# A hybrid four-layer kernel: the rotary halves of queries and keys by DMA instead of by a permutation product

## The chip, the cores and the metric

The kernel runs on one core of a Trainium2 chip. The metric is the device time of one execution in microseconds, over repeated runs. The engines that matter are TensorE (PE, with its weight loads PEld), VectorE (DVE), ScalarE (ACT), GpSimd (POOL) and SyncE (SP), which issues the weight stream. ACT can issue DMAs too, from its own queue.

## The reference, cut to what matters

Two blocks of two layers each, on 256 tokens of width 1024, in float32. The change touches the two layers of the first block, in the attention branch:

```python
def partial_rope(t, cos, sin):
    half = ROT_DIM // 2                    # ROT_DIM = 16, so 8
    t1, t2, rest = tf[..., :half], tf[..., half:ROT_DIM], tf[..., ROT_DIM:]
    out = jnp.concatenate([t1 * c - t2 * s, t2 * c + t1 * s, rest], axis=-1)

for i in range(DEPTH):                     # DEPTH = 2
    h = rmsnorm(x, norm_mix[i])
    proj = h @ w_in[i]
    q, k, v, cb, cc, cx, u, g = jnp.split(proj, IN_SPLITS, axis=-1)
    q = partial_rope(q.reshape(b, l, N_Q_HEADS, HEAD_DIM), cos, sin)   # 8 heads of 64
    k = partial_rope(k.reshape(b, l, N_KV_HEADS, HEAD_DIM), cos, sin)  # 2 heads of 64
    y_attn = sliding_window_attention(q, k, v, attn_sinks[i]) @ w_attn_o[i]
    ...                                    # a convolution branch, a state-space branch, gates, FFN
```

Of the 64 dimensions of each head the first 16 are rotated: the first eight are mixed with the second eight.

## The kernel before, in words

**The weight stream.** All weights pass through as "slabs" of 128 partitions by 1024 columns (512 KB), in the order of use. SP loads a slab into one of four slots of `w_raw`. ACT copies it to `w_hi` (L1310, float32r), DVE computes the rest `w_lo = w_raw - w_hi` (L1811), and PE multiplies with both: 24 products of 128x128 by 128x256 a slab (L777 to L779: high times high, high times low, low times high). ACT and DVE make slab i+3 while they are at position i of their own list, and PE waits for `w_lo` of a slab before its first product. SP reloads a slot when `w_lo` of its slab is made.

**The order of the work.** Each of the first two layers has a table `ORDER1[n]`: after slab i come the tasks listed under i. PE, ACT and DVE each walk the same list in order and do their own share of each task, so the place of a task in the table decides what stands in front of and behind it on every engine. Nothing is reordered at run time.

**The attention part.** Slabs 0 to 4 give four tiles of queries (two heads each) and one of keys; ACT evacuates each into `qk[:, b, :]`, heads along the partitions, tokens along the columns. PE then multiplies each of the five tiles with the matrix `rope_r` (L997, task `("rope", b)`), which puts the turned halves (with their sign) on the first 16 partitions of each head and zeros elsewhere, in a PSUM bank. DVE (task `("rope_mul", b)`, L2146 to L2153) multiplies that with the sine table into `prob[:, b, :]`, the tile itself with the cosine table, and adds the two. `scaled_tables` (L2139) makes both tables, multiplied by the root of the norm, in `prob[:, 5]` and `prob[:, 6]`. Much later PE takes `qk` for the scores.

**Around it on DVE.** In the first layer: `root_of` (L1824 to L1828), the scaled activations (`work`, L1842), their low parts `h_lo` (L1848) and the `w_lo` of coming slabs. The first use of `h_lo` is slab 9 in the first layer and slab 5 in the second (`slab_normed`, L790 to L794: all high parts of x first, then the eight low ones). In the second layer the tasks `("power", p)` (L2115 to L2119) and the convolution (L2280 to L2291) share the same stretch. There is a loop between the engines: at each third slab of the convolution DVE makes `cy` (L2291), ACT makes `cv_hi` of it (L1525), and only then the next `w_hi`, for which DVE waits.

Of the kernel before, what the change touches and what calls it, by code (L numbers as in the profile page):

```python
# [44 lines left out]
SCORE_BANKS = 0, 1, 2  # L45
ROPE_BANKS = 2, 3, 0

# [48 lines left out]
for _name, _n in (("ones_d", P), ("ones_i", P), ("ident", P), ("g_mid", KD), ("g_final", KD),  # L96
                  ("rope_c", T), ("rope_s", T), ("rope_r", P), ("mask", TRI)):
    C1[_name] = (_at, _at + _n)
    _at += _n
# [21 lines left out]
def raw_end(n):  # L121
# [6 lines left out]
        3: (("mean",), ("roots",), ("h", 0), ("h", 1), ("h", 2), ("h", 3), ("lows",)),  # L128
        5: (("rope", 0),),
        6: (("rope", 1),),  # L130
        7: (("prep_d",), ("rope", 2)),
        9: (("scaled",),),
        10: (("rope_mul", 0),),
        12: (("out_table",),),
        14: (("power", 0),),
        15: (("rope", 3), ("rope_mul", 1)),
        17: (("rope", 4),),
        18: (("double", 0), ("double", 1)),
# [31 lines left out]
    },  # L170
    {
        1: (("mean",), ("roots",)),
        3: (("scaled",), ("h", 0), ("h", 1), ("h", 2), ("h", 3), ("lows",)),
        4: (("rope", 0), ("rope_mul", 0), ("rope", 1)),
        5: (("power", 0), ("rope_mul", 1)),
        7: (("rope", 2), ("rope", 3)),
        8: (("rope_mul", 2), ("power", 1)),
        9: (("rope_mul", 3), ("spread", 0), ("rope", 4)),
        10: (("rope_mul", 4), ("vt",), ("vt_copy",)),
        11: (("spread", 1), ("power", 2)),  # L180
# [142 lines left out]
def hybrid_kernel(nc, weights, x_t, p_d, c1_d, c2_d, decay_d, out_t):  # L323
    with ExitStack() as ctx:
# [211 lines left out]
        v_prep = sem("v_prep")  # L536
        pe_rope = sem("pe_rope")
        v_rope = sem("v_rope")
# [193 lines left out]
        def _(pe):  # L732
# [187 lines left out]
            def s5_turned(at, g):  # L920

                part, first = g // 4, 4 * (g % 4)
                if g == 0:
                    pe.wait_ge(v_power, at.n * 3 + 3)
                    pe.wait_ge(a_power, at.n * 2 + 2)
                if g < 4:
                    if g == 1:
                        pe.wait_ge(a_v, at.n + 1)
                    else:
                        pe.wait_ge(v_rope, at.n * 5 + (3, 0, 4, 5)[g])  # L930
                else:
                    pe.wait_ge(a_bt, at.n * 8 + (g - 3))
                for k in range(4):
                    last = nc.tensor.transpose(mid[g % 4][:, k * P:(k + 1) * P],
                                               bs[part][:, first + k, :, :].rearrange("p i c -> p (i c)"), con1("ident"))
                last.then_inc(pe_tr, 1)
# [50 lines left out]

            def rope(at, b):

                wait_out(pe, at, Q0 + b)  # L990
                if b == 0:
                    pe.wait_ge(tables_in, 16)
                if b == 2:
                    pe.wait_ge(v_norm, at.norm * 3 + 1)
                if b >= 3:
                    pe.wait_ge(v_rope, at.n * 5 + (b - 2))
                mm(mid[ROPE_BANKS[b % 3]][:, 0:T], con1("rope_r"), qk[:, b, :],  # L997
                   start=True, stop=True).then_inc(pe_rope, 1)

            def value_rows(at):  # L1000
# [6 lines left out]
            def scores(at, h):  # L1007

                a, g = h // 2, h % 2
                if h == 0:  # L1010
                    pe.wait_ge(v_rot, at.n * 4 + 4)
                elif h >= 3:
                    pe.wait_ge(v_mask, at.n * 8 + (h - 2))
                rows = slice(HD * g, HD * g + HD)
                dst = mid[SCORE_BANKS[h % 3]]
                mm(dst[:, 0:P], qk[rows, a, 0:P], qk[rows, 4, 0:P], start=True, stop=True)
                mm(dst[:, P:TRI], qk[rows, a, P:T], qk[rows, 4, :], start=True, stop=True).then_inc(pe_s, 1)
# [66 lines left out]
            for n in range(DEPTH):  # L1084
                at = Layer(False, n)
                for task in tasks1(n):
                    if task[0] == "slab":
                        first_slab(at, task[1])
                    elif task[0] == "mean":
                        mean(at, 0)  # L1090
                    elif task[0] == "rope":
                        rope(at, task[1])
                    elif task[0] == "tr":
# [210 lines left out]
        def _(act):  # L1304
# [194 lines left out]
            def mixed_high(at, n):  # L1499

                act.wait_ge(v_mg, at.n * 4 + (n + 1))
                nc.scalar.copy(h_hi[:, 2 * n:2 * n + 2, :], work[:, 2 * n:2 * n + 2, :]).then_inc(a_mhi, 1)

            def first_slab(at, i):
                if at.n or i + AHEAD > start_slabs:
# [70 lines left out]
            for n in range(DEPTH):  # L1576
                at = Layer(False, n)
                for task in tasks1(n):
# [12 lines left out]
                    elif task[0] == "lag_copy":  # L1591
                        lag_copy(at, task[1])
                    elif task[0] == "vt_copy":
                        act.wait_ge(pe_v, n + 1)
# [195 lines left out]
        def _(dve):  # L1790
# [355 lines left out]
            def rope(at, own, b):  # L2146

                dve.wait_ge(pe_rope, at.n * 5 + (b + 1))
                cos, sin = prob[:, 5, 0:T], prob[:, 6, 0:T]
                tt(prob[:, b, 0:T], mid[ROPE_BANKS[b % 3]][:, 0:T], sin, MUL)  # L2150
                tt(qk[:, b, :], qk[:, b, :], cos, MUL).then_inc(dve_step, 1)
# [210 lines left out]
            for n in range(DEPTH):  # L2362
                at = Layer(False, n)
                for task in tasks1(n):
# [28 lines left out]
                    elif task[0] == "out_power":  # L2393
                        out_power(at, own, task[1])
                    elif task[0] == "rope_mul":
                        rope(at, own, task[1])
# [508 lines left out]
```

## Time and profile before

| | |
|---|---|
| runs | 2137.98, 2138.44, 2140.2 us; median 2138.44 |
| the profiled execution | 2139.59 us, of which span 2137.80 us (1.79 us around it) |
| PE busy | 2113.5 us, 99% of the span |
| DVE busy | 1640.1 us, 77% |
| ACT busy | 1195.2 us, 56% |
| share of the chain that ended last | PE 89%, DVE 6%, ACT 2%, issue 2% |
| mean granted clock of PE | 0.997 |
| DMA | 385 MB, 180 GB/s over the span |

The busy share of PE is nearly full, since matmuls are pipelined and each is counted from its start to its modelled end. The chain that ended last tells more: it is followed back from the last instruction, at each step to what released it, and so shows in which stretches another engine than PE sets the time.

### The profile page before, as it was taken

Reading aid. Unit: us, or ns where it says so; the run is one execution under the profiler, and the core shown is the slowest. Engines: PE = TensorE matmul, PEld = TensorE weight load, DVE = VectorE, ACT = ScalarE, POOL = GpSimd, SP = SyncE. Lnnn points to the kernel's source line nnn. Section 1 sums busy time; section 2 is a strip of 40 time slices with the busy share of each in tenths; the row PEclk is TensorE's granted clock in tenths of the full one; section 3 lists DMA queues with packets and bytes.
Section 4 is the critical chain, followed back from the end, with each engine's and each line's share of the span. In section 5 each row is a group of like instructions: output and inputs, shape, how many; then the busy total and the mean of one; then the engine's idle time right before and its main releaser. Section 6 shows DMA issues by size and latency. Waiting matters only on the chain.

```text
span 2137.8 us, 47790 instructions
## 1 busy us (share of the span) xinstructions
PE 2113.5 (99%) x18652; PEld 2055.5 (96%) x18652; DVE 1640.1 (77%) x2620; ACT 1195.2 (56%) x1803; POOL 58.5 (3%) x54
## 2 busy tenths in 40 slices
PE   9999999999999999999999999999999999999998
PEld 8999999999999999899999999999899999999998
DVE  8987877987877776778957877776678947877764
ACT  6646644565555445546648745445446658845443
POOL 0000000000000000000002200000000002200000
PEclk9999999999999999999999999999999999999999
DMA  7434655654446556554455566556554556565553
GB/s 251 159 128 141 204 190 186 195 171 142 151 157 215 190 189 206 187 168 158 161 190 191 167 203 208 186 187 213 185 169 148 169 183 193 174 201 186 187 189 127
DMA packets 109984, 385.00 MB, mean 180 GB/s; under 512 B 12480, under 2 KB 16768, under 8 KB 109312
## 3 DMA queue, kind: packets, MB, share of 16 engines
q1 hardware_dynamic: 101664, 368.66, 52.2%
q10 hardware_dynamic: 8160, 14.04, 2.1%
q8 instruction: 121, 1.98, 0.4%
q14 instruction: 39, 0.32, 0.0%
HBM read 381.53 MB, written 1.11 MB: 179 GB/s over the span
## 4 chain that ended last, share of the span: by engine, by line
PE 89%; DVE 6%; ACT 2%; issue 2%; DMA 0%; DVEq 0%; ACTq 0%
PE acc L777 25%; PE acc L779 24%; PE acc L778 24%; DVE w_lo L1811 2%; PE acc L896 1%; PE acc L897 1%; PE acc L898 1%; PE acc L841 1%; PE acc L843 1%; PE acc L842 1%; ACT w_hi L1310 1%; PE mid L1133 1%; PE mid L1214 1%; DVE pr L2564 0%; PE mid L964 0%
## 5 line engine op out<-in xcount | busy, mean ns | idle before, releaser
L1811 DVE TENSOR_TENSOR w_lo<-w_raw,w_hi 128x1024 fp32r<-128x1024 f32 x694 | 848.5, 1227 | 306.8 <-ACT w_hi L1310 297.9
L1310 ACT CAST w_hi<-w_raw 128x1024 fp32r<-128x1024 f32 x694 | 724.7, 1047 | 541.3 <-PE acc L779 473.5
L777 PE MATMUL acc<-h_hi,w_hi 128*128 128x256 f32 x2096 | 599.4, 286 | 0.3 <-DVE w_lo L1811 0.3
L779 PE MATMUL acc<-h_hi,w_lo 128*128 128x256 f32 x2096 | 587.5, 280 | 0.0
L778 PE MATMUL acc<-h_lo,w_hi 128*128 128x256 f32 x2096 | 586.3, 280 | 0.0
L777 PE MATMUL acc<-g_hi,w_hi 128*128 128x256 f32 x1456 | 410.0, 282 | 0.8 <-DVE w_lo L1811 0.7
L779 PE MATMUL acc<-g_hi,w_lo 128*128 128x256 f32 x1456 | 407.2, 280 | 0.0
L778 PE MATMUL acc<-g_lo,w_hi 128*128 128x256 f32 x1456 | 406.8, 279 | 0.0
L777 PEld LDWEIGHTS acc<-h_hi,w_hi 128*128 128x128 f32 x2096 | 395.7, 189 | 7.7 <-issue 5.7
L779 PEld LDWEIGHTS acc<-h_hi,w_lo 128*128 128x128 f32 x2096 | 396.1, 189 | 0.0
L778 PEld LDWEIGHTS acc<-h_lo,w_hi 128*128 128x128 f32 x2096 | 395.1, 188 | 0.5
L777 PEld LDWEIGHTS acc<-g_hi,w_hi 128*128 128x128 f32 x1456 | 274.0, 188 | 2.0 <-DVE w_lo L1811 1.8
L779 PEld LDWEIGHTS acc<-g_hi,w_lo 128*128 128x128 f32 x1456 | 274.4, 188 | 0.0
L778 PEld LDWEIGHTS acc<-g_lo,w_hi 128*128 128x128 f32 x1456 | 273.4, 188 | 0.2
L777 PE MATMUL acc<-f_hi,w_hi 128*128 128x256 f32 x704 | 197.7, 281 | 0.2 <-DVE w_lo L1811 0.2
L779 PE MATMUL acc<-f_hi,w_lo 128*128 128x256 f32 x704 | 196.9, 280 | 0.0
L778 PE MATMUL acc<-f_lo,w_hi 128*128 128x256 f32 x704 | 196.7, 279 | 0.0
L777 PEld LDWEIGHTS acc<-f_hi,w_hi 128*128 128x128 f32 x704 | 132.5, 188 | 0.4 <-issue 0.4
L779 PEld LDWEIGHTS acc<-f_hi,w_lo 128*128 128x128 f32 x704 | 132.7, 188 | 0.0
L778 PEld LDWEIGHTS acc<-f_lo,w_hi 128*128 128x128 f32 x704 | 132.2, 188 | 0.0
L708 POOL TENSOR_TENSOR sqz<-xs 128x256 f32<-128x256 f32 x32 | 36.0, 1134 | 1800.6 <-DVE xs L2557 1800.4
L777 PE MATMUL acc<-r_hi,w_hi 128*128 128x256 f32 x256 | 73.4, 287 | 0.5 <-issue 0.5
(434 smaller groups left out, 3394.3 us busy)
## 6 DMA issues: line engine op xcount, KB each, us to landing
w_raw<-weights_d SPq DMA_DIRECT2D x695, 512.0 KB, 3.9
even<-rows_d ACTq DMA_DIRECT2D x16, 256.0 KB, 4.3
odd<-rows_d ACTq DMA_DIRECT2D x32, 128.0 KB, 3.4
p<-p_d ACTq DMA_DIRECT2D x3, 1080.0 KB, 8.5
rdec<-decay_d ACTq DMA_DIRECT2D x2, 768.0 KB, 5.3
p<-p_d SPq DMA_DIRECT2D x1, 1024.0 KB, 10.7
out_d<-work SPq DMA_DIRECT2D x4, 256.0 KB, 2.3
x_all<-x_d SPq DMA_DIRECT2D x1, 516.0 KB, 4.3
```

Of the source, the lines that this page charges most:

```text
L708: nc.gpsimd.tensor_tensor(sqz[:, b % 4, :], xs[:, b, :], xs[:, b, :], ALU.mult).then_inc(p_zsq, 1)
L777: mm(dst, wh, hi[:, k, :], start=first and j == 0, stop=False)
L778: mm(dst, wh, lo[:, k, :], start=False, stop=False)
L779: done = mm(dst, wl, hi[:, k, :], start=False, stop=last and j == len(ks) - 1)
L841: mm(dst, wh, hi[:, k, :], start=k == 0 and b == 0, stop=False, skip_group_check=True)
L842: mm(dst, wh, lo[:, k, :], start=False, stop=False, skip_group_check=True)
L843: done = mm(dst, wl, hi[:, k, :], start=False, stop=k == 3, skip_group_check=True)
L896: mm(dst, hh, wh, start=k == 0, stop=False)
L897: mm(dst, hh, wl, start=False, stop=False)
L898: done = mm(dst, hl, wh, start=False, stop=k == KD - 1)
L1310: nc.scalar.copy(w_hi[:, slot, :], w_raw[:, slot, :]).then_inc(hi_done, 1)
L1811: tt(w_lo[:, slot, :], w_raw[:, slot, :], w_hi[:, slot, :].bitcast(F32), SUB).then_inc(lo_v, 1)
```

## The change

The five products with `rope_r` of each layer go, and the matrix with them. In their place DVE clears `prob[:, 0:5, 0:256]` (one memset, task `("rope_zero",)`), ACT issues four DMAs (task `("rope_in",)`), each of which copies eight partitions of all five tiles of `qk` to `prob`, eight partitions further down or up. DVE reads the turned half from `prob` in SBUF and no longer from PSUM. The sign goes into the sine table. All five `rope_mul` tasks wait for all four DMAs. In the second layer the `rope_mul` tasks stand later: under slabs 8, 9, 10, 10 and 12, and no longer 4, 5, 8, 9 and 10. In the first layer they stay where they were. Four waits of PE on `v_rope` in `s5_turned` go, and PE's first score waits for it instead.

```diff
@@ ORDER1, first layer
         3: (("mean",), ("roots",), ("h", 0), ("h", 1), ("h", 2), ("h", 3), ("lows",)),
-        5: (("rope", 0),),
-        6: (("rope", 1),),
-        7: (("prep_d",), ("rope", 2)),
+        1: (("rope_zero",),),
+        6: (("rope_in",),),
+        7: (("prep_d",),),
         9: (("scaled",),),
         10: (("rope_mul", 0),),
         12: (("out_table",),),
         14: (("power", 0),),
-        15: (("rope", 3), ("rope_mul", 1)),
-        17: (("rope", 4),),
+        15: (("rope_mul", 1),),
@@ ORDER1, second layer
+        0: (("rope_zero",),),
         1: (("mean",), ("roots",)),
         3: (("scaled",), ("h", 0), ("h", 1), ("h", 2), ("h", 3), ("lows",)),
-        4: (("rope", 0), ("rope_mul", 0), ("rope", 1)),
-        5: (("power", 0), ("rope_mul", 1)),
-        7: (("rope", 2), ("rope", 3)),
-        8: (("rope_mul", 2), ("power", 1)),
-        9: (("rope_mul", 3), ("spread", 0), ("rope", 4)),
-        10: (("rope_mul", 4), ("vt",), ("vt_copy",)),
+        5: (("power", 0), ("rope_in",)),
+        8: (("rope_mul", 0), ("power", 1)),
+        9: (("rope_mul", 1), ("spread", 0)),
+        10: (("rope_mul", 2), ("rope_mul", 3), ("vt",), ("vt_copy",)),
+        12: (("rope_mul", 4),),
@@ PE, s5_turned
-                if g < 4:
-                    if g == 1:
-                        pe.wait_ge(a_v, at.n + 1)
-                    else:
-                        pe.wait_ge(v_rope, at.n * 5 + (3, 0, 4, 5)[g])
-                else:
+                    pe.wait_ge(v_norm, at.norm * 3 + 1)
+                elif g == 1:
+                    pe.wait_ge(a_v, at.n + 1)
+                if g >= 4:
                     pe.wait_ge(a_bt, at.n * 8 + (g - 3))
@@ PE
-            def rope(at, b):
-                ...
-                mm(mid[ROPE_BANKS[b % 3]][:, 0:T], con1("rope_r"), qk[:, b, :],
-                   start=True, stop=True).then_inc(pe_rope, 1)
@@ PE, scores
                 if h == 0:
+                    pe.wait_ge(v_rope, at.n * 5 + 5)
                     pe.wait_ge(v_rot, at.n * 4 + 4)
@@ ACT
+            def rope_rows(at):
+
+                for t in range(U0):
+                    wait_out(act, at, t)
+                act.wait_ge(v_rope_zero, at.n + 1)
+                for base in range(0, P, HD):
+                    for to, off in ((base, ROT // 2), (base + ROT // 2, -(ROT // 2))):
+                        act.dma_start(prob[to:to + ROT // 2, 0:U0, 0:T],
+                                      qk[to + off:to + off + ROT // 2, :, :]).then_inc(rope_in, 16)
@@ DVE, rope
-                dve.wait_ge(pe_rope, at.n * 5 + (b + 1))
+                dve.wait_ge(rope_in, (at.n + 1) * 4 * 16)
                 cos, sin = prob[:, 5, 0:T], prob[:, 6, 0:T]
-                tt(prob[:, b, 0:T], mid[ROPE_BANKS[b % 3]][:, 0:T], sin, MUL)
+                tt(prob[:, b, 0:T], prob[:, b, 0:T], sin, MUL)
@@ DVE, tasks
+                    elif task[0] == "rope_zero":
+                        wait_used(dve, at, 0)
+                        nc.vector.memset(prob[:, 0:U0, 0:T], 0.0).then_inc(v_rope_zero, 1)
```

## Rows read from the trace of the kernel before

**Rows 1.** The page, chain that ended last: share of the span by engine.

```profile
PE 89%; DVE 6%; ACT 2%; issue 2%; DMA 0%; DVEq 0%; ACTq 0%
```

**Rows 2.** Line 997 (the products): count, ns min/median/max, first and last start, form.

```profile
L997 PE MATMUL mid<-qk,c x20: 376/379/380, 27.0 to 460.9; 128*128 128x256 f32 x20
```

**Rows 3.** Timeline of PE, first layer: start us, us, instruction [idle before <-releaser].

```profile
26.86 0.28 PE L779 MATMUL acc<-g_hi,w_lo 128*128 128x256 f32 x1
26.98 0.59 PE L997 MATMUL mid<-qk,c 128*128 128x256 f32 x2
...
27.52 0.28 PE L778 MATMUL acc<-g_lo,w_hi 128*128 128x256 f32 x1
...
30.22 0.60 PE L997 MATMUL mid<-qk,c 128*128 128x256 f32 x2
30.96 0.39 PE L777 MATMUL acc<-g_hi,w_hi 128*128 128x256 f32 x1
```

**Rows 4.** Chain in order of time, 0 to 130 us: start us, us, what.

```profile
29.72 1.20 DVE w_lo L1811
30.96 0.39 PE acc L777
...
89.11 0.48 ACT gate L1315
```

**Rows 5.** Timeline of DVE, first layer, before slab 7.

```profile
19.96 3.49 DVE L1811 TENSOR_TENSOR w_lo<-w_raw,w_hi 128x1024 fp32r<-128x1024 f32 x3
```

**Rows 6.** Timeline of DVE, 59 to 125 us: the nearest memset, and what follows it.

```profile
102.80 1.34 DVE L2125 MEMSET lag<- 128x1536 f32 x1 [0.39 <-DVE turn L2102]
104.06 1.16 DVE L2098 TENSOR_TENSOR turn<-turn 128x1024 f32<-128x1024 f32 x1
```

**Rows 7.** Chain in order of time, 430 to 620 us.

```profile
484.39 1.24 DVE w_lo L1811
485.67 0.39 PE acc L777
```

**Rows 8.** Timeline of DVE, second layer, 425 to 475 us.

```profile
437.30 0.43 DVE L1824 SCALAR_TENSOR_TENSOR rtmp<-mid,rinv 128x256 f32<-128x256 f32 x1 [0.68 <-ACT rinv L1336]
...
440.60 1.23 DVE L1811 TENSOR_TENSOR w_lo<-w_raw,w_hi 128x1024 fp32r<-128x1024 f32 x1 [0.69 <-ACT w_hi L1310]
...
445.70 2.49 DVE L1848 TENSOR_TENSOR h_lo<-work,h_hi 128x512 fp32r<-128x512 f32 x4
...
449.38 0.42 DVE L2150 TENSOR_TENSOR prob<-mid,prob 128x256 f32<-128x256 f32 x1
...
450.50 1.22 DVE L1811 TENSOR_TENSOR w_lo<-w_raw,w_hi 128x1024 fp32r<-128x1024 f32 x1
...
455.93 1.23 DVE L1811 TENSOR_TENSOR w_lo<-w_raw,w_hi 128x1024 fp32r<-128x1024 f32 x1 [0.82 <-ACT w_hi L1310]
```

**Rows 9.** Timeline of DVE, second layer, 473 to 535 us.

```profile
476.17 1.23 DVE L1811 TENSOR_TENSOR w_lo<-w_raw,w_hi 128x1024 fp32r<-128x1024 f32 x1 [1.42 <-ACT w_hi L1310]
```

**Rows 10.** Timeline of ACT, second layer, 425 to 475 us.

```profile
450.28 1.05 ACT L1310 CAST w_hi<-w_raw 128x1024 fp32r<-128x1024 f32 x1
451.60 0.66 ACT L1315 ACTIVATE u<-acc 128x256 f32<-128x256 f32 x1 [0.27 <-PE acc L779]
...
454.41 0.63 ACT L1315 ACTIVATE u<-acc 128x256 f32<-128x256 f32 x1 [1.30 <-PE acc L779]
...
474.78 0.41 ACT L1525 CAST cv_hi<-cy 128x256 fp32r<-128x256 f32 x1 [6.26 <-DVE cy L2291]
```

**Rows 11.** Tile rows_d: DMAs that ACT issues (ns of one issue), and their landing.

```profile
L1668 ACTq DMA_DIRECT2D odd<-rows_d x32: 326/450/969, 1082.7 to 1834.1; - x32
...
DMA to landing us min/median/max: 2.7/3.6/6.4
```

**Rows 12.** Windows: us, busy of PE, PEld, DVE, ACT, POOL; PEclk; DMA.

```profile
102.60:105.50 2.90, 0.19 (x15) 0.03 (x3) 2.70 (x3) 1.29 (x3) 0.00 (x0) 0.90 0.03 6
105.50:111.80 6.30, 6.25 (x51) 5.86 (x53) 3.36 (x4) 3.23 (x5) 0.00 (x0) 0.50 0.09 20
```

More of the change, by code:

```diff
@@ L45 @@
 SCORE_BANKS = 0, 1, 2
-ROPE_BANKS = 2, 3, 0
 N1 = 512 // P
@@ L96 @@
 for _name, _n in (("ones_d", P), ("ones_i", P), ("ident", P), ("g_mid", KD), ("g_final", KD),
-                  ("rope_c", T), ("rope_s", T), ("rope_r", P), ("mask", TRI)):
+                  ("rope_c", T), ("rope_s", T), ("mask", TRI)):
     C1[_name] = (_at, _at + _n)
@@ L536, in hybrid_kernel @@
         v_prep = sem("v_prep")
-        pe_rope = sem("pe_rope")
+        v_rope_zero = sem("v_rope_zero")
+        rope_in = sem("rope_in")
         v_rope = sem("v_rope")
@@ L986, in s5_out @@
                     last.then_inc(pe_y, 1)
-            def rope(at, b):
[L990 to L996, printed above, removed]
-                mm(mid[ROPE_BANKS[b % 3]][:, 0:T], con1("rope_r"), qk[:, b, :],
-                   start=True, stop=True).then_inc(pe_rope, 1)
             def value_rows(at):
@@ L1090, in _ @@
                         mean(at, 0)
-                    elif task[0] == "rope":
-                        rope(at, task[1])
                     elif task[0] == "tr":
@@ L1592, in _ @@
                         lag_copy(at, task[1])
+                    elif task[0] == "rope_in":
+                        rope_rows(at)
                     elif task[0] == "vt_copy":
@@ L2867 @@
     rope_c[:ROT] = np.tile(np.cos(ang).T, (2, 1))
-    rope_s[:ROT] = np.tile(np.sin(ang).T, (2, 1))
+    rope_s[:ROT] = np.concatenate([-np.sin(ang).T, np.sin(ang).T])
     put_c1("rope_c", np.tile(rope_c, (2, 1)))
     put_c1("rope_s", np.tile(rope_s, (2, 1)))
-    turn = np.zeros((P, P), f32)
-    for base in (0, HD):
-        for m in range(half):
-            turn[base + m + half, base + m] = -1.0
-            turn[base + m, base + m + half] = 1.0
-    put_c1("rope_r", turn)
     i, j = np.arange(P)[:, None], np.arange(P)[None]
```

## The prediction, made before the kernel with the change was run

> **What bounds the kernel now.** First I read the shares of the chain that ended last: PE has 89% of it, DVE 6% [rows 1]. So a product taken off PE is worth its full time, except in the stretches where DVE or ACT sets the pace. The whole question is in which of them the ten products stand. For that I read the chain in order of time around the two layers, and then the timelines of PE, DVE and ACT there.
>
> In the first layer the chain is on DVE until 30.92 us, where `w_lo` of slab 7 is ready, and PE begins slab 7 at 30.96 [rows 4]. From there to 89.11 it is on PE, then on ACT. In the second layer there are two stretches that PE doesn't set. Slab 5 can't end before the four `h_lo` pieces are made, 445.70 + 2.49 = 448.19 us [rows 8]; they depend on DVE work that starts at 440.60, when ACT had `w_hi` ready. And from `w_lo` at 455.93 [rows 8] to `w_lo` of slab 18 at 484.39 the chain is on DVE, with a detour over ACT, and PE starts slab 18 only at 485.67 [rows 7]. DVE waits only once in between, 1.42 us before 476.17 [rows 9], and that wait is itself of its own making: ACT waits for DVE's `cy` before it makes `cv_hi` at 474.78 and the next `w_hi` [rows 10].
>
> **What the products cost PE.** There are 20 instructions in the trace, two for each of the ten products [rows 2]. Their durations overlap with the neighbours, so I take the starts: the product starts at 26.98 and L778 of the next slab at 27.52, 0.54 us later, where two neighbouring products start 0.12 us apart (26.86 to 26.98) [rows 3]. One product costs 0.54 - 0.12 = 0.42 us. All ten on the path would be 4.2 us.
>
> - First layer, the first two (26.98 and 30.22): the slab after the second starts at 30.96, with `w_lo`, not with PE [rows 3, 4]. They are worth nothing. The other three (after slabs 7, 15 and 17) stand where the chain is on PE: 3 x 0.42 = 1.26 us gained.
> - Second layer, the first two stand ahead of slab 5, whose end hangs on `h_lo` at 448.19 [rows 8]: nothing. The last three stand at 454.2 and 460.7, after PE has released the `w_hi` from which DVE's stretch begins (ACT's evacuation at 454.41 follows slab 7, ahead of the products [rows 10]), and everything they push is slack until 485.67 [rows 7]: nothing.
>
> **The memset.** 128x1280 elements. The nearest row clears 1536 columns and the next instruction starts 104.06 - 102.80 = 1.26 us later [rows 6]; by columns that is 1.05 us. Bounds: 0 (if it ran beside the neighbour) and 1.26 us. In the first layer it comes after the first of the three `w_lo` that start at 19.96 [rows 5]. From there DVE has no wait until 30.92, so `w_lo` of slab 7, and slab 7, come 1.05 us later; slabs 5 and 6 keep their cover (the third `w_lo`, of slab 6, is done at 19.96 + 3.49 = 23.45, its slab starts after the product of 26.98). In the second layer it comes ahead of two waits of DVE, 0.68 us before 437.30 and 0.69 us before 440.60 [rows 8], 1.37 us together: hidden. If that cover were gone, it would be 1.05 us there too.
>
> First layer: +1.05 - 1.26 = -0.2 us. DVE then carries its 1.05 us on; from 31 to 89 us PE never waits for a `w_lo` in the chain [rows 4], and by their starts the smallest lead (slab 28) is about 1.5 us, so it decides nothing. What is late next is the start of the transposes (they wait for the last `power`), and they are held by ACT's copies right after.
>
> **The moved work of DVE, second layer.** One `rope_mul` takes 450.50 - 449.38 = 1.12 us of DVE [rows 8]. That its first operand is now in SBUF changes nothing that the rows would let me see (0.42 us from PSUM, 0.41 from SBUF, of the same shape; bounds -0.1 to +0.1 us for all). Before, two of the five were done ahead of 455.93, where DVE then sat idle 0.82 us [rows 8]; three lay in its stretch. Now the one under slab 12 falls in the idle 1.42 us behind `cy` [rows 9], but four lie ahead of that `cy`. So DVE's stretch is one `rope_mul` longer: +1.12 us. PE is faster by 3 x 0.42 us in that stretch, then waits for `w_lo` from slab 15 on, and slab 18 starts later by what DVE is later. Bounds: 0 if ACT's next `w_hi` doesn't follow, 2.24 if the one under slab 12 isn't hidden either. I take 1.12.
>
> **The four issues on ACT.** An issue takes 0.45 us in the median, 0.33 at least [rows 11]; four with their six waits make some 1.9 us. In the first layer ACT has no work there for over 2 us. In the second they stand ahead of `w_hi` at 450.28; ACT's waits behind it, 0.27 and 1.30 us, take up 1.57 [rows 10]. What is left, 0.3 us, delays the `w_hi` on which DVE's stretch starts. Bounds 0 and 1 us. Queued behind ACT here are only that `w_hi` and two evacuations whose banks are wanted three slabs later.
>
> **The copies themselves.** 40 KB each, 160 rows of 1 KB for the four. DMAs from the same queue land 2.7 to 6.4 us after the issue, 3.6 in the median [rows 11]. In the second layer the last is issued at about 451.8, lands at 455.4, and the first `rope_mul` is due at 457.3: cover of about 2 us. In the first layer it is over 8 us. Cost nothing; at 6.4 us it would be 0.9 us. The queue of SP is not touched, but four 512 KB slabs are in flight or near it in that time.
>
> **Sum.** -0.2 (first layer) + 1.12 + 0.3 (second) = +1.2 us. The profiled execution took 2139.59 us, 1.79 around its span of 2137.80; it becomes 2140.8. That execution lies 1.15 above the median of the runs, so the median goes from 2138.44 to 2139.6. The second block is not touched, and PE sets its pace as before.
>
> **Rivals.**
> - *The products count in full.* The stretch 455.93 to 485.67 isn't lengthened because DVE catches up on the way, and the memset hides: gain up to ten times 0.42 = 4.2 us, time 2134.2. For it: PE is busy for 99% and DVE for 77%. Against: DVE's rows there show one wait, and two products of the first layer stand directly in front of a wait for DVE. Half way (only the second layer's DVE cost missing), it is 2138.2.
> - *The copies come late.* If four transfers on eight partitions don't run side by side, they take 4 x 3.6 = 14.4 us from 450.4, land at 464.8, 7.5 us after they are wanted, and DVE's stretch is late by that: 2147.1. It decides from 2 us over the median landing. For it: the same queue, few partitions, and no row of before shows a transfer of eight partitions. Against: 1 KB rows to 128 partitions, of the same queue and issued in pairs, land in 3.6 us. The Trainium skill, "DMA: Bandwidth & Descriptors", section "Why a DMA increments its semaphore by 16 and not by 1", says that a DMA is spread over the largest number of engines up to 16 that divides its outermost dimension. By that rule eight engines would carry all four copies and eight stand by, which speaks for this rival; no run here has shown it.
> - *The stalls for instructions on PE* (2.9 us at 102.6 [rows 12], 1.8 at 498.4) move, since PE's stream is 40 instructions shorter: 1 us either way. It is in the forecast's own range.
>
> **How the numbers follow.** Forecast 0.60 (2139.6, own range 2138 to 2141.5), products in full or half way 0.15, clock 0.13, late copies 0.12. Runs of before lie 2.2 us apart. 0.2% is 4.3 us, about what can be told from no change: faster means below 2134.2, slower above 2142.7. The first rival just touches the one, the clock just the other, late copies lie beyond it. Faster 0.07, same 0.73, slower 0.20. Range 2135.0 to 2143.5.
>
> **What would show it.** L997 gone; slab 7's first L777 at 32.0, not 30.96; ACT's gate after slab 26 within 0.3 us of 89.11. In the second, slab 5's end as before; `cy` of slab 12 and `w_lo` of slab 18 1.1 to 1.5 us later against slab 5; PE waiting for `w_lo` at slabs 15 to 18. The copies landed ahead of the first `rope_mul`, so that DVE's wait for them is nil. Wrong would be: DVE idle in 456 to 474, a gain at slab 18, a wait of DVE for a DMA, or a second stretch of the clock at 0.5.

## The result and the profile after

The changed kernel takes 2141.56 us (median of 12 runs, 2138.86 to 2143.23), the kernel before 2138.44 us (median of 12, 2135.66 to 2140.20). The ratio is 1.0018, with a 95% interval of [1.0010, 1.0025]: slower by 3.1 us in the medians, 2.1 to 5.3 us by the interval. The forecast was 2139.6, the range 2135.0 to 2143.5. The time lies inside the range. The change of +1.2 us that was forecast lies below the interval of the measured change. Timed again, the ratio was 1.0014 [1.0005, 1.0023], a mean difference of 3.0 us.

The profiled execution took 2142.86 us, its span 2141.0 (before: 2139.59 and 2137.80). The page first; the chain's shares answer to [rows 1].

```profile
span 2141.0 us, 47760 instructions
PE 2111.0 (99%) x18632; PEld 2052.5 (96%) x18632; DVE 1643.1 (77%) x2622; ACT 1195.1 (56%) x1803; POOL 58.5 (3%) x54
PE 88%; DVE 8%; ACT 2%; issue 2%; DMA 0%; ACTq 0%; DVEq 0%
```

PE has lost the 20 instructions of [rows 2] and 2.5 us of busy time, and yet the time is longer. DVE's share of the chain goes from 6 to 8%. The chain in order of time shows where: before it was on PE from 31 to 89 us [rows 4], now it leaves PE at 69 us, and DVE is in it from 70.3 to 96.8.

```profile
31.03 1.20 DVE w_lo L1807
...
69.14 1.04 ACT w_hi L1294
70.28 1.23 DVE w_lo L1807
...
90.10 0.70 DVE bs_im L2115
...
96.10 0.69 DVE bs_im L2115
96.84 3.71 PE mid L931 x32
```

**First layer.** The timelines of DVE and of PE around slab 7 (start us, us, instruction, [idle before <-releaser]):

```profile
21.42 1.12 DVE L2393 MEMSET prob<- 128x1280 f32 x1 [0.21 <-issue]
22.46 2.29 DVE L1807 TENSOR_TENSOR w_lo<-w_raw,w_hi 128x1024 fp32r<-128x1024 f32 x2
```

```profile
29.69 0.28 PE L778 MATMUL acc<-g_hi,w_lo 128*128 128x256 f32 x1
32.27 0.38 PE L776 MATMUL acc<-g_hi,w_hi 128*128 128x256 f32 x1 [2.30 <-DVE w_lo L1807]
```

The memset takes 22.46 - 21.42 = 1.04 us and 0.21 of idleness comes ahead of it, and slab 7 starts at 32.27 where it was 30.96 [rows 4]: +1.31. ACT evacuates slab 26 at 89.25, 0.14 after the 89.11 of [rows 4]. Up to there the three products (1.26) and the memset (1.31) balance. But the next thing that PE does is to transpose the results of DVE's last `power` (L931, before L934), and there the two traces part. Before, then after:

```profile
95.08 1.97 PE L934 MATMUL mid<-c,bs_re 128*128 128x128 f32 x16 [0.37 <-DVE bs_im L2119]
97.92 2.12 PE L934 MATMUL mid<-c,bs_im 128*128 128x128 f32 x16 [0.87 <-ACT bt L1452]
```

```profile
96.84 1.97 PE L931 MATMUL mid<-c,bs_re 128*128 128x128 f32 x16 [1.64 <-DVE bs_im L2115]
98.64 1.91 PE L931 MATMUL mid<-c,bs_im 128*128 128x128 f32 x16
```

DVE never made up its lateness, and it had grown. Against the end of `w_lo` of slab 4, `w_lo` is 1.28 us later than before at slabs 5 to 9, 1.69 at slab 10 and 1.72 to 1.73 from there to slab 29. What came in at slab 10 is a wait for ACT, whose `w_hi` stands behind the last three of the four issues:

```profile
31.95 2.55 ACTq L1495 DMA_DIRECT2D prob<-qk  x3
34.61 1.05 ACT L1294 CAST w_hi<-w_raw 128x1024 fp32r<-128x1024 f32 x1 [2.30 <-issue]
```

```profile
35.70 1.23 DVE L1807 TENSOR_TENSOR w_lo<-w_raw,w_hi 128x1024 fp32r<-128x1024 f32 x1 [0.21 <-ACT w_hi L1294]
```

DVE's last `bs_im` starts at 96.10 and no longer at 94.34, 1.76 us later, and PE waits 1.64 us for it. Behind it a wait of 0.87 us for ACT is gone. The first of the 256 small products after the transposes (L961, before L964) starts at 102.53 instead of 102.01. So the first layer has cost 0.5 us when its gain was expected to be 0.2.

**Second layer.** ACT's timeline with its queue's issues, then DVE's; the DVE rows answer to [rows 8, 9].

```profile
450.51 0.74 ACTq L1495 DMA_DIRECT2D prob<-qk  x1
...
451.29 2.15 ACTq L1495 DMA_DIRECT2D prob<-qk  x3
453.53 1.05 ACT L1294 CAST w_hi<-w_raw 128x1024 fp32r<-128x1024 f32 x1 [1.65 <-PE acc L778]
```

```profile
454.62 1.22 DVE L1807 TENSOR_TENSOR w_lo<-w_raw,w_hi 128x1024 fp32r<-128x1024 f32 x1 [2.53 <-ACT w_hi L1294]
...
457.48 1.23 DVE L1807 TENSOR_TENSOR w_lo<-w_raw,w_hi 128x1024 fp32r<-128x1024 f32 x1 [0.23 <-ACT w_hi L1294]
458.62 0.42 DVE L2146 TENSOR_TENSOR prob<-prob 128x256 f32<-128x256 f32 x1
...
477.03 0.41 DVE L2287 TENSOR_TENSOR cy<-ccx,acc 128x256 f32<-128x256 f32 x1
...
478.87 1.23 DVE L1807 TENSOR_TENSOR w_lo<-w_raw,w_hi 128x1024 fp32r<-128x1024 f32 x1 [0.29 <-ACT w_hi L1294]
```

The four issues hold ACT for 2.9 us here, not the 1.9 assumed (in the first layer they run from 30.61 to 34.50, around one `w_hi`). The first `rope_mul` (458.62) follows `w_lo` without a gap, so it waits for no DMA. `cy` comes at 477.03, and behind it DVE's old wait of 1.42 us [rows 9] has shrunk to 0.29, since the fifth `rope_mul` fills it. PE's waits from 430 to 500 us (total, times, longest):

```profile
PE acc L776 <- DVE w_lo L1807: 1.6, 2, 1.4
PE mid L931 <- DVE bs_im L2115: 0.5, 1, 0.5
```

The kernel before has a single one there, of 0.3 us. To take the layer by itself I compare how much later `w_lo` ends at slab 18 of the layer than at its slab 0: +1.21 us against before. One `rope_mul` is 1.12 of it [rows 8].

**The rest of the difference isn't steady.** In this trace, between 102 and 180 us, PE stands for stalls with the releaser "issue" (it waits for nothing that the profile shows), and the clock falls for some microseconds, as it does before. The columns are those of [rows 12], the granted clock the last but two; the first two rows are of the kernel before and of a second trace of the same kernel before:

```profile
104.90:111.70 6.80, 6.15 (x47) 5.83 (x47) 3.96 (x5) 3.81 (x6) 0.00 (x0) 0.50 0.08 17
```

```profile
106.20:109.60 3.40, 3.40 (x19) 3.40 (x18) 2.14 (x4) 2.69 (x4) 0.00 (x0) 0.50 0.03 5
```

```profile
105.70:109.10 3.40, 3.39 (x24) 3.22 (x25) 2.95 (x4) 3.29 (x7) 0.00 (x0) 0.51 0.03 5
```

The third is of the changed kernel. The same program lost 3.4 us (6.8 at half speed) in one execution and 1.7 in another. The stalls move too, but they aren't longer in the changed kernel: over the whole span PE's waits with the releaser "issue" add up to 7.4 and 7.9 us in the two traces of before, and to 8.3, 7.5 and 6.6 in three of the changed kernel. This is why a single pair of traces says nothing on a difference of 2 or 3 us in this stretch, and why what follows goes by medians and by places ahead of it or within the second layer.

### The profile page after: what moved, and what is told of

The parts are those of the page before. It is cut to its first block, busy times and chain, and to the rows that moved or that the text cites. A ratio compares the mean times of both kernels' runs of the same rounds, so it can differ in the third digit from the quotient of the medians.

```text
span 2141.0 us, 47760 instructions
## 1 busy us (share of the span) xinstructions
PE 2111.0 (99%) x18632; PEld 2052.5 (96%) x18632; DVE 1643.1 (77%) x2622; ACT 1195.1 (56%) x1803; POOL 58.5 (3%) x54
## 4 chain that ended last, share of the span: by engine, by line
PE 88%; DVE 8%; ACT 2%; issue 2%; DMA 0%; ACTq 0%; DVEq 0%
PE acc L776 25%; PE acc L778 24%; PE acc L777 24%; DVE w_lo L1807 3%; PE acc L895 1%; PE acc L896 1%; PE acc L897 1%; PE acc L840 1%; PE acc L842 1%; PE acc L841 1%; ACT w_hi L1294 1%; PE mid L1117 1%; PE mid L1198 1%; DVE pr L2563 0%; PE mid L961 0%
```

## The experiments

e7 and e8 are second traces of the two kernels, and e11 gives a third one of the changed kernel. Two positions are read from each trace, both against the first trace of before and free of each run's own start (the end of `w_lo` of slab 4): A, the first small product after the transposes of the first layer; B, `w_lo` of slab 18 of the second layer against that of its slab 0. "Clock" is the mean granted clock over the timed executions minus that of the kernel before in the same comparison; 0.001 of it over 2138 us is 2.1 us. "Idle" is the time from the start of PE's last product before slab 7 to the start of its first one. "Fall" says whether the clock falls right behind slab 7 in the trace. The mean differences are known to about 1 us (1.4 for e6), the clock differences to 0.0004 to 0.0006 (95%, from the scatter of the executions), which is also about 1 us.

```
                      median   ratio to before            mean diff  clock     A      B    idle before slab 7, fall
before                   -       -                          -         -       0      0     0.5  no
changed               2141.56  1.0018 [1.0010, 1.0025]    +3.3        -      +0.5  +1.21   2.6  no
e11_after_timed       2140.38  1.0014 [1.0005, 1.0023]    +3.0     -0.0010   +1.6  +1.39   2.6  yes
e1_zero_pool          2137.93  1.0006 [0.9997, 1.0015]    +0.9     -0.0003   -0.8  +1.67   1.3  no
e2_order              2142.49  1.0025 [1.0016, 1.0035]    +5.4     -0.0012   +0.4  +2.17   2.6  no
e3_fill               2139.72  1.0013 [1.0004, 1.0022]    +2.6     -0.0009   +1.5  +1.18   2.6  yes
e4_no_products        2135.74  0.9993 [0.9984, 1.0002]    -1.1     -0.0003   -1.2  +0.05   1.3  no
e5_late               2140.05  1.0014 [1.0005, 1.0024]    +2.7     -0.0007   -1.3  -0.22   1.3  no
e6_before_fill        2139.37  1.0005 [0.9996, 1.0014]    +1.7     -0.0002    0.0  -0.01   0.5  no
e9_pool_all           2138.71  1.0007 [0.9998, 1.0016]    +1.3     -0.0005   -1.2  +1.14   1.3  no
e10_pool_late         2136.74  0.9996 [0.9987, 1.0005]    -0.9     -0.0008   -1.2  -1.65   1.3  no
e12_pool_issue        2141.92  1.0017 [1.0008, 1.0026]    +3.9     -0.0012   +1.6  +1.18   2.6  yes
e7_before_again       2139.39  one execution                                  0.0  +0.02   0.5  no
e8_after_again        2139.60  one execution                                 +1.6  +1.20   2.6  yes
```

B has a weakness: in e1 and e11 a part of it arises ahead of the four issues and of the `rope_mul`. In e1 `w_lo` of slab 2 waits 2.26 us for ACT where it waited 1.41 in the kernel before, and is 0.69 us later for it. At `w_lo` of slab 7 the changed kernel is level with before (0.02 us), and the issues have delayed nothing yet. Counted from there to slab 18, the cost is 1.15 in e1, 1.14 in e9, 1.16 in e12 and 1.17 to 1.19 in the four traces with memset and issues as in the changed kernel (changed, e3, e8, e11); it is 2.15 in e2, -0.22 in e5, -1.65 in e10 and 0.03 in e4. I call this B from slab 7.

**e1_zero_pool: the memset on GpSimd.**

```diff
+            for n in range(DEPTH):
+                wait_used(pool, Layer(False, n), 0)
+                nc.gpsimd.memset(prob[:, 0:U0, 0:T], 0.0).then_inc(v_rope_zero, 1)
@@ DVE
-                    elif task[0] == "rope_zero":
-                        ...
```

> The kernel after, with the two memsets done by GpSimd and not by DVE. My theory (DVE sets the start of slab 7, and the memset stands in that line): slab 7's first product is back at 30.9 to 31.1 us (after: 32.27, before: 30.96), w_lo of slabs 10 to 28 of the first layer is 1.3 us earlier than after, and the second layer up to slab 18 is unchanged against its own slab 5. Median 1 to 1.3 us under the kernel after, about 2140.3, unless the stalls inside the state-space part change. Rival (only stalls for instructions and the clock make the difference to before): slab 7 may be early, but the median doesn't move.

PE's first product of slab 7, from its timeline:

```profile
31.38 0.38 PE L779 MATMUL acc<-g_hi,w_hi 128*128 128x256 f32 x1 [1.01 <-DVE w_lo L1810]
```

This run starts 0.42 us later as a whole, so slab 7 is back at its old place (31.38 - 0.42 = 30.96). A falls from +0.5 to -0.8: the memset on DVE costs 1.3 us in the first layer, and it costs them at the transposes. The median ratio falls from 1.0018 to 1.0006. In the mean that is some 2 us, more than the 1.3 of slab 7; the clock, lower than before's by 0.0003 here and by 0.0010 in e11, can hold the rest.

**e2_order: `rope_mul` of the second layer at nearly its old places.**

```diff
-        5: (("power", 0), ("rope_in",)),
-        8: (("rope_mul", 0), ("power", 1)),
-        9: (("rope_mul", 1), ("spread", 0)),
-        10: (("rope_mul", 2), ("rope_mul", 3), ("vt",), ("vt_copy",)),
+        4: (("rope_in",),),
+        5: (("power", 0),),
+        7: (("rope_mul", 0), ("rope_mul", 1)),
+        8: (("rope_mul", 2), ("power", 1)),
+        9: (("rope_mul", 3), ("spread", 0)),
+        10: (("vt",), ("vt_copy",)),
```

> The kernel after, with the DMAs of the second layer issued one slab earlier and rope_mul 0 and 1 under slab 7, 2 and 3 under 8 and 9, 4 under 12 (after: 8, 9, 10, 10, 12). My theory (four rope_mul lie in DVE's stretch from w_lo of slab 11 to cy of slab 12 where there were three): w_lo of slabs 15 to 18 comes 1.1 to 1.5 us earlier against slab 5 than after, median 1 to 1.5 us lower, about 2140.2. Rival (the 2.9 us of DMA issues on ACT delay w_hi and set the stretch, wherever the rope_mul stand): w_lo of slab 18 stays within 0.3 us of after.

ACT's queue, then DVE:

```profile
448.95 2.92 ACTq L1497 DMA_DIRECT2D prob<-qk  x4
451.97 1.05 ACT L1296 CAST w_hi<-w_raw 128x1024 fp32r<-128x1024 f32 x1 [3.21 <-issue]
```

```profile
453.06 1.23 DVE L1809 TENSOR_TENSOR w_lo<-w_raw,w_hi 128x1024 fp32r<-128x1024 f32 x1 [2.50 <-ACT w_hi L1296]
455.50 1.22 DVE L1809 TENSOR_TENSOR w_lo<-w_raw,w_hi 128x1024 fp32r<-128x1024 f32 x1 [1.22 <-ACT w_hi L1296]
...
458.05 0.42 DVE L2148 TENSOR_TENSOR prob<-prob 128x256 f32<-128x256 f32 x1
...
460.31 1.22 DVE L1809 TENSOR_TENSOR w_lo<-w_raw,w_hi 128x1024 fp32r<-128x1024 f32 x1
```

A miss: B is +2.17 and not less than +1.21, and this is the slowest kernel of all. Issued one slab earlier, the 2.92 us of issues stand ahead of four `w_hi`, DVE idles 2.50 + 1.22 us, and only then come two `rope_mul`, ahead of `w_lo` of slab 11. To move DVE's work forward was worth nothing here, with ACT's issues in front of the `w_hi` that DVE then waits for. The run moved both, so it doesn't price either alone.

**e3_fill and e6_before_fill: only PE's stream of instructions made longer.** In e3 25 semaphore increments a layer stand where the products were; in e6 the kernel before gets twelve after slab 11 and twelve after slab 13 of its first layer.

```diff
+                    elif task[0] == "fill":
+                        for _ in range(task[1]):
+                            pe.sem_inc(filler, 1)
```

> The kernel after, with 25 instructions on PE in each of the first two layers that only count up a semaphore nobody waits for, at the places of the removed products, so that PE's stream is about as long as before. It adds nothing to DVE, ACT or the DMAs. Theory of moved stalls: the three long gaps of 1.06, 0.76 and 0.91 us in PE's s5_out part of the first layer (167 to 177 us) give way to one of about 0.84 as before, so w_lo of slab 51 is 1.5 to 2.5 us earlier than after; median near 2139.6. Rival (the gaps come from something else, such as ACT or DVE being late): they stay, and the fillers add 0 to 1 us.

> The kernel before, with 24 instructions on PE in the first layer (12 after slab 11, 12 after slab 13) that only count up a semaphore nobody waits for. Nothing else is changed. Theory (PE's stalls for instructions depend on where its stream stands): up to slab 27 every start is within 0.3 us of before, and then in the state-space part (94 to 180 us) the sizes or places of the gaps change by 0.5 us or more, by w_lo of slabs 33 to 51; the second layer's gaps change likewise. Rival (gaps come from semaphores of other engines): the gaps keep places and sizes within 0.2 us.

In e6 nothing but the filler is different. Its trace has a stall in the middle of a slab that the first trace of before doesn't have. But the second trace of before (e7) has one at the same product, only shorter. The stall of e6 first, then that of e7:

```profile
115.86 0.39 PE L781 MATMUL acc<-h_lo,w_hi 128*128 128x256 f32 x1 [1.72 <-issue]
```

```profile
115.69 0.39 PE L778 MATMUL acc<-h_lo,w_hi 128*128 128x256 f32 x1 [0.69 <-issue]
```

So it isn't shown that the filler moved a stall. e6's mean is 1.7 us over before, and its interval holds 1; its "issue" waits add up to 7.7 us, as before's do. In e3 three stalls (0.84, 0.55 and 0.63 us idle, between 168 and 178 us) are gone, but they are gone from e11 too, whose program has no filler. The mean of e3 is 2.6 over, against 3.0 and 3.3 for the unfilled kernel. The rival that moved stalls make the whole 3 us isn't supported, by these runs or by the sums of the waits; what smaller part they could make is open.

**e4_no_products: before without the products.** Each product becomes four semaphore increments and DVE multiplies the sine table with `qk` itself. It leaves the turned halves out.

> The kernel before, with each product with the permutation matrix replaced by four instructions of PE that only count up semaphores, and DVE multiplying the sine table with the tile itself: the turned halves are left out, the rest is computed. My theory (three of ten products lie on the path, all in the first layer): w_lo of slab 20 to 28 of the first layer unchanged, PE 1.2 to 1.3 us earlier at the end of slab 26, slab 18 of the second layer not earlier against slab 5; median 1.0 to 1.5 us under before, about 2137.2. Rival (all ten count): 4.2 us under before, about 2134.2.

A is -1.2, B +0.05. ACT's evacuation of slab 26, which follows PE, starts at 87.99, 0.12 of which is the run's later start: 1.24 us earlier than before's 89.11. So the three products of the first layer are worth 1.24 us up to there, and the second layer's five nothing, as predicted. At the transposes PE waits for DVE all the same (columns: busy us, mean ns | idle before):

```profile
L935 PE MATMUL mid<-c,bs_re 128*128 128x128 f32 x16 | 2.0, 276 | 1.6 <-DVE bs_im L2121 1.6
```

The first half of the transposes starts no earlier than before. What is kept at A is that ACT, 1.24 us earlier too, no longer holds up the second half (0.87 us of wait in the kernel before). That A is the price of the three products once more is in part luck: a larger gain would have been kept back by DVE's `bs_im`. All ten products together are worth 1.1 us in the mean (the ratio's interval reaches from 3.4 us to nothing), where 4.2 was the price by count.

**e5_late: the tasks where ACT and DVE stood idle.** First layer: memset under slab 10, issues under 14, all five `rope_mul` at slabs 28 and 29. Second layer:

```diff
-        5: (("power", 0), ("rope_in",)),
-        8: (("rope_mul", 0), ("power", 1)),
+        5: (("power", 0),),
+        8: (("power", 1), ("rope_in",)),
...
+        12: (("rope_mul", 0),),
+        15: (("rope_mul", 1),),
+        18: (..., ("rope_mul", 2), ("rope_mul", 3), ("rope_mul", 4)),
```

> The kernel after, with the three kinds of tasks put where ACT and DVE stood idle in the trace before. First layer: rope_zero under slab 10, rope_in under 14, rope_mul 0 at the end of 28, 1 to 4 at the head of 29. Second layer: rope_in under 8, rope_mul 0 under 12, 1 under 15, 2 to 4 under 18. My theory (the change lost what it freed on PE because memset and rope_mul lie in stretches that DVE sets): slab 7 starts at 30.96; the end of slab 26 of the first layer is 1.2 us earlier than before; slab 18 of the second layer starts 1.5 to 1.8 us earlier than before and 2.7 to 3.0 earlier than after, both against slab 5. Median 3 us under before and 5 to 6 under after, that is 2134 to 2136, if the stalls in the state-space parts stay as large. Rival (the copies or the issues on ACT cost what is lost): slab 18 isn't earlier than before, or rope_mul waits for a DMA, and the median stays above before.

ACT's queue in the second layer, DVE behind it, and PE's longest wait from 60 to 182 us:

```profile
458.39 3.04 ACTq L1492 DMA_DIRECT2D prob<-qk  x4
461.54 1.05 ACT L1291 CAST w_hi<-w_raw 128x1024 fp32r<-128x1024 f32 x1 [2.71 <-PE acc L775]
```

```profile
462.69 1.23 DVE L1804 TENSOR_TENSOR w_lo<-w_raw,w_hi 128x1024 fp32r<-128x1024 f32 x1 [0.97 <-ACT w_hi L1291]
465.67 1.22 DVE L1804 TENSOR_TENSOR w_lo<-w_raw,w_hi 128x1024 fp32r<-128x1024 f32 x1 [1.76 <-ACT w_hi L1291]
```

```profile
PE mid L999 <- DVE tm L2158: 2.3, 1, 2.3
```

A miss. In the second layer DVE has 3.4 us less to do ahead of `cy`, and nearly all of it goes in waits for the `w_hi` behind the issues (the two shown and a third of 0.27: 3.0 us). In the first layer A is -1.3, as good as without memset and products, and is given back 15 us later, where PE waits 2.3 us for DVE, which the five `rope_mul` have made late.

**e9_pool_all and e10_pool_late: nothing of the change on ACT.** Memset and issues on GpSimd; e10 has besides e5's places of `rope_mul` in the second layer.

```diff
+                for t in range(U0):
+                    wait_out(pool, at, t)
+                pool.wait_ge(v_rope_zero, at.n + 1)
+                ...
+                        pool.dma_start(prob[to:to + ROT // 2, 0:U0, 0:T], ...).then_inc(rope_in, 16)
@@ ACT
-                    elif task[0] == "rope_in":
-                        rope_rows(at)
```

> The changed kernel with the memset and the four DMA issues of each layer on GpSimd, which has no other work there; ACT keeps nothing of the change. Theory (the 2.9 us that the four issues take of ACT delay the w_hi of slabs 8 to 11 and so DVE): with ACT free again w_lo of slab 11 comes as in the kernel before, and only the rope_mul that stands one more ahead of cy is left. w_lo of slab 18 of the second layer against that of its slab 0: 1.1 us later than in the kernel before, where the version with only the memset on GpSimd has 1.67. First layer: slab 7 as before, 1.3 us gained by slab 18. Sum about 0 against the kernel before: 2138, and 0.6 under the version with the memset alone on GpSimd. Rival 1 (the issues on ACT hide in its waits): 1.6 to 1.7 stays. Rival 2 (DMAs issued by GpSimd are slower: issue or landing): the first rope_mul waits for them in the second layer, DVE shows a wait there, and slab 18 is 2 us or more late.

> As the kernel with memset and issues on GpSimd, and in the second layer the five rope_mul stand under slabs 12, 15 and 18 (three), as in the late version, whose gain there was eaten by 0.97, 1.76 and 0.27 us in which DVE waited for w_hi behind the four issues on ACT. Theory: with the issues off ACT these waits fall to about 1 us together, no rope_mul stands ahead of cy of slab 12 where the kernel before had three (3.4 us of DVE, of which its 1.42 us wait behind cy gives nothing back), so w_lo of slab 18 comes 1.5 to 2.5 us earlier than in the kernel before: about 2136.5, the first version under the kernel before. Rival 1 (DVE's work there isn't the bound once it is thinned, PE and ACT follow at once): 0 to -0.5 at slab 18, 2138. Rival 2: the three rope_mul under slab 18 push the next w_lo, so that the gain is given back by slab 25: -2 at slab 18 and 0 from 25 on, 2138.

The issues by their line (ns of one, min/median/max, and us to landing), on GpSimd in e9 and on ACT in the changed kernel; then DVE ahead of `w_lo` of slab 11 in e9:

```profile
L727 POOL DMA_DIRECT2D prob<-qk x8: 577/577/740, 30.2 to 446.4; - x8
...
DMA to landing us min/median/max: 2.4/3.5/4.6
```

```profile
L1495 ACTq DMA_DIRECT2D prob<-qk x8: 696/700/1312, 30.6 to 452.7; - x8
```

```profile
452.21 1.23 DVE L1816 TENSOR_TENSOR w_lo<-w_raw,w_hi 128x1024 fp32r<-128x1024 f32 x1 [1.57 <-ACT w_hi L1305]
```

In e9 B is +1.14, the 1.1 of the expectation: what is left is one `rope_mul` (1.12 us by [rows 8]). But this doesn't show that ACT's issues cost anything: the +1.67 of e1, against which the expectation was set, has half a microsecond from before the issues, and from slab 7 e1 and e9 cost the same (1.15 and 1.14). At the places that the changed kernel gives to `rope_mul`, the issues on ACT hide in the second layer, which was rival 1. In the first layer they show: `w_lo` of slab 10 is 0.40 us late in e1 and 0.01 in e9. In e10 DVE's rows read:

```profile
461.44 1.23 DVE L1818 TENSOR_TENSOR w_lo<-w_raw,w_hi 128x1024 fp32r<-128x1024 f32 x1
463.87 1.23 DVE L1818 TENSOR_TENSOR w_lo<-w_raw,w_hi 128x1024 fp32r<-128x1024 f32 x1 [1.20 <-ACT w_hi L1307]
465.37 1.23 DVE L1818 TENSOR_TENSOR w_lo<-w_raw,w_hi 128x1024 fp32r<-128x1024 f32 x1 [0.27 <-ACT w_hi L1307]
```

Two waits where e5 has three, 1.5 us where it has 3.0, and B is -1.65 us (expected -1.5 to -2.5), and still is at slab 24. The same places of `rope_mul` gave only -0.22 with the issues on ACT (under slab 8, in e5): there those issues cost 1.4 us, since DVE isn't the bound any more. e10 is the fastest version that computes all, at 2136.74 us against 2137.62 for before in the same comparison; the ratio's interval [0.9987, 1.0005] doesn't tell it from before.

**e11_after_timed, e12_pool_issue: the clock behind slab 7.** e11 is the changed kernel once more. e12 is e9 with the memset back on DVE.

> The changed kernel once more, timed against the kernel before on one chip with the granted clock of every execution. The traces give the change +0.14 us up to 89 us and +1.21 in the second layer, 1.35 us in all; its median is 3.1 later. Theory: the rest is the clock. PE stands idle for 2.57 us ahead of slab 7, and in some executions (two of four traces with that gap) the granted clock falls for 3.4 us behind it, which costs 1.7 us; other falls come as before. Then the mean granted clock over the executions is 0.0006 to 0.0013 lower than that of the kernel before (each 0.001 of the mean over 2138 us is 2.1 us), and the time difference minus that is 1.4 us, within 0.8. Rival (stalls of PE on its instructions are longer with the changed stream): the clocks are equal within 0.0003 and the 3 us stay.

> The four issues on GpSimd as in the kernel with all of it there, but the memset on DVE as in the changed kernel: the gap ahead of slab 7 is 2.57 us again, the second layer as with all on GpSimd (+1.1 at slab 18, the memset being hidden there). Theory: against the kernel with all on GpSimd (mean 1.3 us over the kernel before, clock 0.0005 lower) slab 7 costs 1.2 to 1.3 us and the clock that falls behind the gap in some executions 0.6 to 1.7: 3.2 to 4.2 us over the kernel before by itself, but if ACT's issues only cost the 0.1 us that the second layer shows, the same as the changed kernel within 1 us: about 2140.5. Rival (the gap costs only itself): 2.6 over the kernel before, clock as with all on GpSimd.

The same 3.4 us in the first trace of the changed kernel and in e11's (granted clock again the last figure but two):

```profile
32.40:35.80 3.40, 3.40 (x30) 3.40 (x31) 3.19 (x5) 1.05 (x1) 0.00 (x0) 1.00 0.68 202
```

```profile
32.40:35.80 3.40, 3.40 (x18) 3.40 (x19) 3.16 (x5) 1.05 (x1) 0.00 (x0) 0.52 0.72 197
```

18 products instead of 30 in the same time. Of the six traces with PE idle for 2.6 us ahead of slab 7, four have the fall (e3, e8, e11, e12); of the eight with 0.5 or 1.3 us, none. Where it falls, A is +1.5 to +1.6 instead of +0.4 to +0.5: of the 1.7 us lost at half clock 1.1 arrive, since PE would have waited for DVE at the transposes anyway (e8 waits 0.69 us there, the changed kernel's first trace 1.64). Over the timed executions the clock of e11 is 0.0010 lower than that of before, so by the arithmetic 2.1 of its 3.0 us, give or take 0.8, are time at the lower clock; the fall behind slab 7 is 1.1 of them if the traces are typical (1.7 in two executions of three). What remains, 0.9, was expected as 1.4, within 0.8. e12 less 2.6 us of clock leaves 1.3. Against e9, from which it differs in the memset alone, it is 3.9 - 1.3 = 2.6 us slower in the mean (each against its own runs of before), where the memset's own 1.3 us would have been the rival's answer. The 95% interval of that 2.6 is about 1.0 to 4.1, so the means alone don't decide it; the count of falls in the traces is the better evidence.

The clock is lower by 0.0005 and 0.0008 in e9 and e10 as well, which have only 1.3 us ahead of slab 7 and no fall behind it. Take A (+0.5 where the trace has the fall), B from slab 7, and the clock difference times 2138 us, and add them: the sums are 0.9 for e9 (measured 1.3), -1.1 for e10 (-0.9), 5.2 for e2 (5.4), 1.0 for e1 (0.9), 3.7 for e11 (3.0) and 4.3 for e12 (3.9), and all versions but e5, whose wait of 2.3 us lies behind A, are met within 1.2 us, which is about the noise. So what A and B leave open goes with a lower mean clock, but not with slab 7 alone: where else the clock falls more often than in the kernel before, and why, stays open.

## Why the prediction's range held, and where its steps failed

The time, 2141.56 us, lies within 2135.0 to 2143.5, and what was held most likely, a change of under 0.2%, came true (0.18%). The forecast change was +1.2, the measured one +3.1: the wide range holds it, and the sum does not.

**Held.** One product costs 0.42 us, three of the first layer count (1.24 us at slab 26 in e4) and the second layer's five don't (B: +0.05 in e4). The memset sets slab 7 later, as predicted, by 1.31 us where 1.05 was put down (it adds 1.04 and 0.21 of idleness ahead of it), and is hidden in the second layer: e9 and e12 differ by it alone and have B of 1.14 and 1.18. One `rope_mul` more in DVE's stretch costs 1.12 (e9: 1.14). That its operand is now in SBUF changes nothing: the first operation takes 0.42 us from either. PE waits for `w_lo` at slabs 15 and 18 of the second layer, and the copies are there in time.

**The step that failed: "from 31 to 89 us PE never waits for a `w_lo` in the chain ..., so it decides nothing".** That was true up to 89 us, and the gate at 89.25 passed the test that I had set. But DVE had next to no slack from 20 to 95 us (before: one wait of 0.30 us for ACT ahead of 60.9; now 0.29 at the same place and the 0.21 ahead of 35.7), so its lateness travelled through, grew by 0.4 us behind ACT's issues at slab 10, and came due at the transposes as 1.76 us. I named them as the next thing late and put the wait down to ACT's copies. In the rows of before both are there, 0.37 us for DVE first and 0.87 for ACT behind; DVE's is the one that ends last now. The first layer's -0.2 is +0.5.

**Mis-sized: the issues.** 0.72 us each, not 0.45, and 2.9 us for the four. The rows that I went by were transfers of another shape, of 128 partitions, 0.33 us at least and 0.45 in the median [rows 11]. The 0.3 us that I gave them in the second layer isn't there, although they are longer than I thought: from slab 7 the layer costs the same with the issues on ACT and on GpSimd (1.15 in e1 and 1.14 in e9 without the memset on DVE, 1.19 in the changed kernel and 1.16 in e12 with it). That B's +1.2 comes near the predicted 1.4 is therefore the one `rope_mul` alone. They cost 1.4 us where the `rope_mul` are gone from DVE's stretch (e5 against e10). In the first layer, where I gave them nothing because ACT has no work for over 2 us, they take 3.9 us with a `w_hi` between them, and cost 0.4 us at A (e1 against e9).

**The clock rival, given 0.13 as a world of its own, is a part of the true case.** Its place was right. The idle time from start to start was 2.6 us where 2.3 was predicted. Its price was not right: 1.7 us at half clock in place of 3.15, 1.1 after the transposes, in four of six traces. If that share holds for all executions, it is 0.7 us of the mean.

**The other rivals.** Products in full: refuted by e4. Late copies: the issues on GpSimd landed in 2.4 to 4.6 us, and in the changed kernel no `rope_mul` waited. That a DMA of eight partitions is carried by fewer engines, as the Trainium skill has it ("DMA: Bandwidth & Descriptors", section "Why a DMA increments its semaphore by 16 and not by 1"), is not contradicted by this. No run here shows how many engines carried a copy. At 40 KB, whatever it costs, the first `rope_mul` never waited for it.

**The sum now.** First layer +0.5, second +1.2, the fall behind slab 7 +0.7: 2.4 us, where the two measurements have 3.0 and 3.3 in the mean, known to about 1 us. The first two terms are shown at their places. The third rests on a count of six traces. The rest is open: other falls of the clock differ from execution to execution (e11 loses 2.1 us more to the clock than before, and slab 7 explains 1.1 of it).

## What to carry to other kernels

An engine that is busy without a gap carried its added time on over 65 us here, however far ahead of the consumer it seemed to be; look for the next place where the bounding engine needs its *last* result, not only its next one. An operation that is swapped for a DMA costs the issuing engine its issues: here four issues of 8 partitions with 5 rows of 1 KB were dearer than the rows of another transfer had said, and moved to an idle engine (GpSimd) they cost nothing that the traces show. When a position is compared between traces, check that the difference arises behind the point where the change begins: e1's B had half a microsecond from ahead of it. Work that came off the bounding engine is worth its time only where no other engine sets the pace: here 1.2 us of 4.2. And a second trace of the unchanged kernel is the cheapest control: it had the stall that one would have blamed on the filler.

## What the runs showed of the hardware that I had not expected

- A DMA issue on ACT took 0.70 us in the median for 8 partitions of 5 rows of 1 KB, and 1.31 for the first, against 0.33 at least and 0.45 in the median for transfers to 128 partitions [rows 11]; on GpSimd the same took 0.58.
- The same 2.6 us from start to start brings a fall of the clock in some executions (four of six) and none in others, and 0.5 or 1.3 us brought none in eight traces; within the kernel a fall lasted 3.4 us, or 6.8 once, at 1.2 GHz.
- Executions of one program differ by 5 us (2134.7 to 2140.2 for before on one chip), and a part of that goes with the clock: the 95 executions of before timed beside the experiments took 2136.4, 2137.6 and 2139.2 us in the mean at a mean clock of 0.999, 0.998 and 0.997. That is 1.4 us for 0.001, less than the 2.1 of the arithmetic.
- GpSimd clears 128x1280 float32 in 1.17 us, about as fast as DVE (1.12).
